# A third Strassen tile pair in the gate projections of a float32 decoder layer, and an earlier start for the first

## The chip, the cores and the metric

The kernel runs on one core of a Trainium2 chip. The metric is the device time of one execution in microseconds (us). Of the kernel before there are three timed runs: 1432.1 us in the median, 1432.09 to 1432.28. Its profiled execution took 1433.02 us, of which the span from the first to the last instruction is 1431.2 us.

## The reference, cut to what matters

All of it is float32, with SEQ = 256 tokens and D_MODEL = 2048. The change lies in the joint projection (its last two parts, the gates) and in how the merge uses them:

```
h = rms_norm(x, ln_mix_w[i])
proj = h @ w_in[i]                      # (256, 2048) @ (2048, 9216)
u_pool, q, f_logit, inp, g, gate_a, gate_b = jnp.split(proj, split_idx, axis=-1)
y_a = multiscale_pool(u_pool, ...) @ w_branch_a[i]
y_b = hgrn2(q, f_logit, inp, g, ...) @ w_branch_b[i]
merged = jax.nn.sigmoid(gate_a) * y_a + jax.nn.sigmoid(gate_b) * y_b
x = x + merged @ w_out[i]
```

After it come a convolutional feed-forward block (`w_up`, `w_down`), a gated embedding (`w_ple_gate`, `w_ple`) and a final norm. Factors in `setup_inputs` scale some of the inputs; they change no shape.

## The kernel before, in words

**Units.** The weights stream through a ring of four buffers (`raw`, `w_hi`, `w_lo`, RING = 4). One *unit* is two row tiles of 128 rows by 512 columns, 512 KB. SyncE issues its DMA; ScalarE rounds it into `w_hi` (`split_hi`, L1119); VectorE subtracts, for the remainder `w_lo` (`split_lo`, L1421); TensorE then takes for each row tile and each of the two blocks of 128 tokens three matmuls, hi x hi, hi x lo and lo x hi (`triple`, L717 to L721; `row_tile`, L661 to L663), 12 in all.

**Slots.** ScalarE's and VectorE's programs are written out slot by slot. In slot s they first split unit s + 3, and then do whatever else is due in that slot, in the order in which it stands in `slot`. A split of unit s + 3 waits until TensorE is through with unit s - 1, whose buffer it takes. Nothing is reordered by a scheduler: each engine works its list in order and waits at semaphores.

**The merge stage.** It has four passes n = 0 to 3 over 512 columns each. A pass from n = 1 on has 24 units, which the text counts from 0 within the pass: units 0 to 15 are the gates (row tile pair i = 0 to 7, for each pair unit 2i of gate a and unit 2i + 1 of gate b), 16 to 19 are branch a, 20 to 23 branch b. The gates accumulate in the PSUM tensor `main`, the branches in `aux`.

**Strassen's scheme.** A tile pair with both gates is a 2 x 2 block product: 2 blocks of tokens, 2 row tiles, 2 column groups. Plain, it takes 8 block products. For the pairs in `GATES_AT` the kernel takes 7 (the Winograd form). Three of them come with the units themselves (`gate_seven`, L789), four use sums of weight tiles and come one pair later (`gate_weight_sums`, L803). The first halves of these follow unit 2i + 2, the second halves unit 2i + 3. Of the products, four (`gate_product`) are gathered over the pairs in the four banks of `aux`: the first is written by `gate_seven`, the second and third (`gate_product(1)` and `(3)`) in the bank pair `aux[0]`. Before the first product of a pass TensorE waits for `gated` (L797), because VectorE must have read branch b's result of the pass before out of `aux`, and before the second for `mT_ready` (L810), because `aux[0]` also holds the transposed `m` of the pass before.

**The sums.** In slot 2i - 2 VectorE forms the four sums of weight tiles in three instructions (`weight_diffs`, L1666, L1668, L1670); ScalarE rounds them in two halves (L1274), and VectorE subtracts in two halves (`sums_lo`, L1695) in the slots 2i and 2i + 1. In these slots the unit 2i + 1 has only one row tile to split (L1117, L1418), since the other is used in sums alone. The sums of activation blocks do not depend on n. They are formed once per pair, during pass 0: GpSimd joins hi and lo (`join_parts`, L2001), VectorE adds four times (`act_sums`), ScalarE rounds and VectorE subtracts. They lie in a buffer with two places.

**Between the passes.** In slot 0 of a pass VectorE multiplies branch b's result with the sigmoid (L1818) and adds both branches to `m_tok` (L1823). TensorE transposes `m_tok` into `aux[0]` after unit 2 (`turn_m`, L714, eight small matmuls). In slot 3 ScalarE copies it out as `mT_hi` (L1331), and VectorE subtracts for `mT_lo` (L1826), which raises `mT_ready`.

**The combination.** When the last Strassen pair is through, ScalarE copies the first product out (L1294), and VectorE makes the shared sums in four additions (`combine_gates`, L1703), then adds them to `main` (`sum_gates`, L1726). TensorE waits for the first of the four before branch a (unit 16), and for all of them before branch b (unit 20).

Of the kernel before, what the change touches and what calls it, by code (L numbers as in the profile page):

```python
# [29 lines left out]
ALU = mybir.AluOpType  # L30
ACT = mybir.ActivationFunctionType
AX_X = mybir.AxisListType.X
F32 = mybir.dt.float32
# [3 lines left out]
P = 128  # L37
# [3 lines left out]
KD = D // P  # L41
# [12 lines left out]
NQ = D // NCOL  # L54
# [8 lines left out]
UK = KD // 2  # L63
# [3 lines left out]
MIX = 10 * UK  # L67
WOUT = MIX + NQ * 2 * (UK + UB)
UP = WOUT + NQ * UK
DOWN = UP + NUP * UK  # L70
# [53 lines left out]


SEVEN_AT = ((5, 8, 11, 14, 17), (5, 8, 11, 14, 17))
GATES_AT = (2, 4)
N_GATES = len(GATES_AT) * (NQ - 1)
SEVENS = [gate_unit(n, i) for n in range(1, NQ) for i in GATES_AT] + [down_unit(p, i) for p in range(2) for i in SEVEN_AT[p]]
SEVEN = {u: q for q, u in enumerate(SEVENS)}  # L130
ACT_SUMS = [0, 1] + SEVENS[N_GATES:]
SUMS_AT = {max(u - 4, DOWN + UK) if f > 1 else MIX + 2 * UK - 2 + 3 * f: f for f, u in enumerate(ACT_SUMS)}
N_SEVEN = [N_GATES + len(SEVEN_AT[0]), len(SEVENS)]
COMBINED0 = 4 * (NQ - 1)

# [66 lines left out]
GATES_COMBINE_AT = [gate_unit(n, GATES_AT[-1]) + 5 for n in range(NQ)]  # L202
# [19 lines left out]
def build(nc, x, x_t, p_t, vecs, convs, w_in, pool_mix_w, w_branch_a, w_branch_b, w_out, w_up, w_down,  # L222
          w_ple_gate, w_ple, ln_final_w, ident_c, levels_c, counts_c, out):
    with ExitStack() as ctx:
# [3 lines left out]
        def sb(name, shape, dt=F32, where=ctx):  # L228
# [63 lines left out]
        mT_hi = sb("mT_hi", [P, KD, SEQ], F32R, mg)  # L292
        mT_lo = sb("mT_lo", [P, KD, SEQ], F32R, mg)
# [15 lines left out]
        a_sums = sb("a_sums", [P, 2, SEQ], F32, ffn)  # L309
        a_sums_hi = sb("a_sums_hi", [P, 2, 4, P], F32R, ffn)  # L310
        a_sums_lo = sb("a_sums_lo", [P, 2, 4, P], F32R, ffn)
# [60 lines left out]
        w_diffs, w_summed, w_sums_hi_ready, w_sums_ready, w_sums_done = map(  # L372
            sem, ("w_diffs", "w_summed", "w_sums_hi_ready", "w_sums_ready", "w_sums_done"))
# [40 lines left out]
        def sums_parts(q):  # L414

            if q < N_GATES:
                return gate_sums_hi, gate_sums_lo
            return w_sums_hi, w_sums_lo

        def down_acc(n, tb):  # L420

# [180 lines left out]
        def _(pe):  # L602
# [121 lines left out]
                return aT_hi[:, k, tb * P:(tb + 1) * P], aT_lo[:, k, tb * P:(tb + 1) * P]  # L724

            def act_sum(q, k):
                return a_sums_hi[:, q % 2, k, :], a_sums_lo[:, q % 2, k, :]

            def ring_tile(u, t):
                return w_hi[:, u % RING, t, :], w_lo[:, u % RING, t, :]  # L730
# [15 lines left out]
            def down_seven(u, p, i, a):  # L746

                q = SEVEN[u - a]
                first, end = i == SEVEN_AT[p][0], i == SEVEN_AT[p][-1]
                pe.wait_ge(lo_full, u + 1)  # L750
                if a == 0:
                    if first:
                        if p:
                            pe.wait_ge(xT_ready, 4 * (2 * NQ + 2))
                        else:
                            pe.wait_ge(z_read, NUP + 1)
                    triple(product(p, 0), *act_block(2 * i, 0), *ring_tile(u, 0), start=first, stop=end)
                    mm = triple(down_acc(2 * p, 0), *act_block(2 * i + 1, 0), *ring_tile(u, 1), start=False, stop=False)
                else:
                    pe.wait_ge(a_sums_ready, q + 3 - N_GATES)  # L760
                    mm = triple(down_acc(2 * p + 1, 0), *act_sum(q, 2), *ring_tile(u, 1), start=False, stop=False)
                mm.then_inc(units_done, 1)

# [25 lines left out]
            def gate_seven(u, n, i, a):  # L789

                q = SEVEN[u - a]
                first, end = i == GATES_AT[0], i == GATES_AT[-1]
                pe.wait_ge(lo_full, u + 1)
                if a == 0:
                    if first:
                        pe.wait_ge(gated, 4 * n)
                    triple(gate_product(0), *x_block_t(2 * i, 0), *ring_tile(u, 0), start=first, stop=end)  # L797
                    mm = triple(main[:, 0, 0, :], *x_block_t(2 * i + 1, 0), *ring_tile(u, 1), start=False, stop=False)
                else:
                    pe.wait_ge(a_sums_ready, q % 2 + 1)  # L800
                    mm = triple(main[:, 1, 0, :], *act_sum(q, 2), *ring_tile(u, 1), start=False, stop=False)
                mm.then_inc(units_done, 1)

# [172 lines left out]
            u = 0  # L976
            first_unit()
            u = 1
# [65 lines left out]
            u = DOWN  # L1044
# [62 lines left out]
        def _(ac):  # L1107
# [153 lines left out]
            def sums_hi(q, part):  # L1261

                if part == 0:
                    ac.wait_ge(a_summed, q + 1)
                    if q > 1:
                        ac.wait_ge(w_sums_done, 2 * (q + N_GATES - 3))
                    ac.activation(a_sums_hi[:, q % 2].rearrange("p k t -> p (k t)"), a_sums[:].rearrange("p k t -> p (k t)"),
                                  ACT.Copy).then_inc(a_sums_hi_ready, 1)
                else:
                    half = part - 1  # L1270
                    ac.wait_ge(w_summed if half else w_diffs, 2 * (q + 1) if half else q + 1)
                    if q:
                        ac.wait_ge(w_sums_done, 2 * (q - 1) + half + 1)
                    ac.activation(sums_parts(q)[0][:, 2 * half:2 * half + 2, :], w_sums[:, 2 * half:2 * half + 2, :],  # L1274
                                  ACT.Copy).then_inc(w_sums_hi_ready, 1)
# [134 lines left out]
        def _(dve):  # L1410
# [274 lines left out]
            def sums_lo(q, part):  # L1685

                if part == 0:
                    dve.wait_ge(a_sums_hi_ready, q + 1)
                    dve.tensor_tensor(a_sums_lo[:, q % 2].rearrange("p k t -> p (k t)"), a_sums[:].rearrange("p k t -> p (k t)"),
                                      a_sums_hi[:, q % 2].rearrange("p k t -> p (k t)").bitcast(F32), ALU.subtract).then_inc(a_sums_ready, 1)  # L1690
                else:
                    half = slice(2 * (part - 1), 2 * part)
                    dve.wait_ge(w_sums_hi_ready, 2 * q + part)
                    hi, lo = sums_parts(q)
                    dve.tensor_tensor(lo[:, half, :], w_sums[:, half, :], hi[:, half, :].bitcast(F32),  # L1695
                                      ALU.subtract).then_inc(w_sums_ready, 1)
# [3 lines left out]
            def add_up(out, a, b):  # L1700

                combines[0] += 1
                return dve.tensor_tensor(out, a, b, ALU.add).then_inc(combined, 1)  # L1703

            def combine_gates(n, part):

                p5, p6, p7 = (gate_product(k) for k in range(1, 4))
                t = [w_sums[:, k, :] for k in range(4)]
                if part == 0:
                    dve.wait_ge(copied, n)  # L1710
                    dve.wait_ge(m_ready, n)
                    add_up(sig_b[:, 1, :], p6, t[0])
                    dve.wait_ge(combined, combines[0])
                    add_up(t[1], p5, sig_b[:, 1, :])
                if part == 1:
                    add_up(t[2], p7, sig_b[:, 1, :])
                    dve.wait_ge(combined, combines[0])
                    add_up(t[3], p5, t[2])
# [35 lines left out]
                    add(x_tok[:, 1, c1], x_tok[:, 1, c1], t[3])  # L1754

            def slot(s):
                if s < UK - LEAD:
                    half_lo(s + LEAD)
                    x_lo(s + LEAD)
                else:  # L1760
                    split_lo(s + LEAD)
                if s in SUMS_AT:
                    act_sums(SUMS_AT[s])
# [6 lines left out]
                        sums_lo(SEVEN[s - k], k + 1)  # L1770
                for n in range(1, NQ):
                    if GATES_COMBINE_AT[n] <= s < GATES_COMBINE_AT[n] + 2:
                        combine_gates(n, s - GATES_COMBINE_AT[n])
                    for k in range(2):
                        if s == merge_slot(n, k) + 1:
                            sum_gates(n, k)
# [168 lines left out]
        def _(pool):  # L1945
# [39 lines left out]
                pool.wait_ge(g_ready, 2 * (g + 1))  # L1985
                pool.tensor_tensor(dec[:, 0, :], dec[:, 0, :], g_tok[:].rearrange("p b n -> p (b n)"), ALU.mult).then_inc(o_gated, 1)

            def join_parts(f, u):

                if f < 2:  # L1990
                    k, hi, lo = 2 * GATES_AT[f], xT_hi, xT_lo
                else:
                    k, hi, lo = u - DOWN - 2 * UD * (u >= DOWN + 2 * UD), aT_hi, aT_lo
                if f == 2:
                    pool.wait_ge(aT_ready, NUP)
                if f:
                    pool.wait_ge(a_sums_ready, f)
                else:
                    pool.wait_ge(yaT_ready, 8)
                    pool.wait_ge(obT_ready, 8)  # L2000
                pool.tensor_tensor(a_sums[:], hi[:, k:k + 2, :].bitcast(F32), lo[:, k:k + 2, :].bitcast(F32),  # L2001
                                   ALU.add).then_inc(a_joined, 1)
# [3 lines left out]
                pool.wait_ge(conv2, plus(j + 1, 1, it))  # L2006
                pool.tensor_tensor(act[:, 0:nf, :], cv[:, 0:nf, :], cv[:, nf:2 * nf, :], ALU.mult).then_inc(prod_u, 1)  # L2007

            for f in range(2):
                join_parts(f, 0)  # L2010
            root(1)
            product(0, 1)
            with pool.Fori(0, NUP - 1) as it:
                product(1, 2, it)
            for f, u in enumerate(ACT_SUMS[2:], 2):
                join_parts(f, u)
            root(2)
            for tb in range(TB):
                pool.wait_ge(end_ms, tb + 1)
# [48 lines left out]
```

## Time and profile before

| | |
|---|---|
| median of 3 runs | 1432.1 us |
| profiled execution | 1433.02 us, span 1431.2 us |
| TensorE (PE) busy | 1420.7 us, 99% |
| PE weight loads busy | 1207.4 us, 84% |
| VectorE (DVE) busy | 1033.4 us, 72% |
| ScalarE (ACT) busy | 774.3 us, 54% |
| GpSimd (POOL) busy | 171.5 us, 12% |
| moved by DMA | 273.47 MB, 191 GB/s in the mean |

Matmuls overlap: a row gives one from its start to its end, and the next starts before that. The distance of their starts tells the pace, not the duration. The same holds, to a smaller degree, for two instructions of VectorE or ScalarE in a row of which neither waits. Idle time in brackets is that of the engine ahead of the instruction, with what ended it.

### The profile page before, as it was taken

Reading aid. Unit: us, or ns where it says so; the run is one execution under the profiler, and the core shown is the slowest. Engines: PE = TensorE matmul, PEld = TensorE weight load, DVE = VectorE, ACT = ScalarE, POOL = GpSimd, SP = SyncE. Lnnn points to the kernel's source line nnn. Section 1 sums busy time; section 2 is a strip of 40 time slices with the busy share of each in tenths; the row PEclk is TensorE's granted clock in tenths of the full one; section 3 lists DMA queues with packets and bytes.
Section 4 is the critical chain, followed back from the end, with each engine's and each line's share of the span. In section 5 each row is a group of like instructions: output and inputs, shape, how many; then the busy total and the mean of one; then the engine's idle time right before and its main releaser. Section 6 shows DMA issues by size and latency. Waiting matters only on the chain.

```text
span 1431.2 us, 19783 instructions
## 1 busy us (share of the span) xinstructions
PE 1420.7 (99%) x7094; PEld 1207.4 (84%) x7094; DVE 1033.4 (72%) x1284; ACT 774.3 (54%) x937; POOL 171.5 (12%) x115
## 2 busy tenths in 40 slices
PE   9999999999999999999999999999999999999997
PEld 7888888888888888888888888888888888888886
DVE  7676777867577765566777777777777888887755
ACT  7555655545454544455555555555555555555644
POOL 0044144100000000000111101111011110000000
PEclk9999999999999999999999999999999999999999
DMA  9655555455665665466656566565665555566663
GB/s 323 199 176 162 161 170 169 147 189 193 193 204 177 220 236 189 156 206 185 190 176 205 177 191 194 173 204 181 192 193 180 202 197 194 174 197 215 231 200 121
DMA packets 190876, 273.47 MB, mean 191 GB/s; under 512 B 11744, under 2 KB 103136, under 8 KB 190688
## 3 DMA queue, kind: packets, MB, share of 16 engines
q1 hardware_dynamic: 190384, 272.30, 59.4%
q8 instruction: 38, 0.62, 0.2%
q10 hardware_dynamic: 432, 0.37, 0.1%
q14 instruction: 22, 0.18, 0.0%
HBM read 270.53 MB, written 2.10 MB: 190 GB/s over the span
## 4 chain that ended last, share of the span: by engine, by line
PE 97%; DVE 1%; issue 0%; DMA 0%; ACT 0%; SPq 0%; ACTq 0%; POOLq 0%; POOL 0%; DVEq 0%
PE aux L839 11%; PE main L839 11%; PE main L661 10%; PE main L663 10%; PE main L662 10%; PE aux L848 6%; PE main L848 6%; PE main L719 5%; PE main L720 5%; PE main L721 5%; PE aux L719 3%; PE aux L720 3%; PE aux L721 3%; PE aux L662 2%; PE aux L661 2%; PE aux L663 2%
## 5 line engine op out<-in xcount | busy, mean ns | idle before, releaser
L1421 DVE TENSOR_TENSOR w_lo<-raw,w_hi 128x1024 fp32r<-128x1024 f32 (+1 forms) x484 | 596.8, 1244 | 337.8 <-ACT w_hi L1119 337.4
L1119 ACT ACTIVATE w_hi<-raw 128x1024 fp32r<-128x1024 f32 (+1 forms) x484 | 508.6, 1052 | 517.3 <-PE main L663 158.4
L661 PE MATMUL main<-w_hi,xT 128*128 128x512 f32 x510 | 201.4, 395 | 0.5 <-DVE w_lo L1883 0.3
L662 PE MATMUL main<-w_lo,xT 128*128 128x512 f32 x510 | 198.6, 389 | 0.0
L663 PE MATMUL main<-w_hi,xT 128*128 128x512 f32 x510 | 198.5, 389 | 0.0
L839 PE MATMUL aux<-xT,w_hi 128*128 128x512 f32 x704 | 169.8, 391 | 0.0
L839 PE MATMUL main<-xT,w_hi 128*128 128x512 f32 x672 | 163.0, 391 | 0.0
L839 PEld LDWEIGHTS aux<-xT,w_hi 128*128 128x128 f32 x704 | 129.3, 188 | 25.3 <-issue 0.3
L839 PEld LDWEIGHTS main<-xT,w_hi 128*128 128x128 f32 x672 | 123.2, 188 | 23.6
L2007 POOL TENSOR_TENSOR act<-cv 128x512 f32<-128x512 f32 (+1 forms) x22 | 71.9, 3267 | 418.8 <-DVE cv L1645 418.8
L661 PEld LDWEIGHTS main<-w_hi,xT 128*128 128x128 f32 x510 | 95.8, 188 | 20.3 <-DVE xT L1448 1.3
L663 PEld LDWEIGHTS main<-w_hi,xT 128*128 128x128 f32 x510 | 95.7, 188 | 20.0
L662 PEld LDWEIGHTS main<-w_lo,xT 128*128 128x128 f32 x510 | 95.9, 188 | 18.8
L848 PEld LDWEIGHTS aux<-xT,w_lo 128*128 128x128 f32 x704 | 90.3, 191 | 3.4
L848 PE MATMUL aux<-xT,w_lo 128*128 128x256 f32 x704 | 91.3, 283 | 0.0
L848 PEld LDWEIGHTS main<-xT,w_lo 128*128 128x128 f32 x672 | 86.4, 191 | 3.5
L848 PE MATMUL main<-xT,w_lo 128*128 128x256 f32 x672 | 87.5, 283 | 0.0
L1645 DVE SCALAR_TENSOR_TENSOR cv<-z,convT,cv 128x255 f32<-128x255 f32 (+1 forms) x172 | 71.7, 479 | 3.0
L1948 POOL TENSOR_TENSOR st<-st,minus_half 128x2 f32<-128x2 f32 (+1 forms) x5 | 3.2, 645 | 490.1 <-DVE st L1479 359.1
L719 PE MATMUL main<-w_hi,xT 128*128 128x512 f32 x150 | 58.6, 391 | 0.0
L721 PE MATMUL main<-w_hi,xT 128*128 128x512 f32 x150 | 58.4, 389 | 0.0
L720 PE MATMUL main<-w_lo,xT 128*128 128x512 f32 x150 | 58.4, 389 | 0.0
(305 smaller groups left out, 2115.3 us busy)
## 6 DMA issues: line engine op xcount, KB each, us to landing
raw<-in_w_up SPq DMA_DIRECT2D x336, 256.0 KB
raw<-in_w_in SPq DMA_DIRECT2D x136, 512.0 KB
raw<-in_w_down SPq DMA_DIRECT2D x84, 512.0 KB
raw<-in_w_out SPq DMA_DIRECT2D x32, 512.0 KB
raw<-in_w_ple_gate SPq DMA_DIRECT2D x32, 512.0 KB
raw<-in_w_branch_a SPq DMA_DIRECT2D x16, 512.0 KB
raw<-in_w_branch_b SPq DMA_DIRECT2D x16, 512.0 KB
raw<-in_w_in SPq DMA_DIRECT2D x15, 256.0 KB, 5.9
```

The lines of the kernel that those rows point to most:

```text
L661: pe.matmul(acc, th, wh, start=first, stop=False)
L662: pe.matmul(acc, th, wl, start=False, stop=False)
L663: return pe.matmul(acc, tl, wh, start=False, stop=end)
L719: pe.matmul(acc, th, wh, start=start, stop=False)
L720: pe.matmul(acc, th, wl, start=False, stop=False)
L721: return pe.matmul(acc, tl, wh, start=False, stop=stop)
L839: mm = pe.matmul(up_acc(j, b), w_hi[:, u % RING, a, b * P:(b + 1) * P], xT[:, k, :, :].rearrange("p h t -> p (h t)"), start=(k == 0), stop ...
L848: mm = pe.matmul(up_acc(j, b)[:, 0:SEQ], w_lo[:, u % RING, a, b * P:(b + 1) * P], xT[:, k, 0, :], start=False, stop=False)
L1119: ac.activation(w_hi[:, u % RING, :, 0:w], raw[:, u % RING, :, 0:w], ACT.Copy).then_inc(hi_full, 1)
L1421: dve.tensor_tensor(w_lo[:, u % RING, :, 0:w], raw[:, u % RING, :, 0:w], w_hi[:, u % RING, :, 0:w].bitcast(F32), ALU.subtract).then_inc(lo ...
L1645: last_op = dve.scalar_tensor_tensor(out=cv[:, b, d:SEQ], in0=z[:, b, 0:SEQ - d], scalar=convT[:, tap, f0(f)], in1=cv[:, b, d:SEQ], op0=AL ...
L2007: pool.tensor_tensor(act[:, 0:nf, :], cv[:, 0:nf, :], cv[:, nf:2 * nf, :], ALU.mult).then_inc(prod_u, 1)
```

## The change

`GATES_AT` becomes (1, 3, 5) instead of (2, 4). So each of the passes 1, 2 and 3 takes three tile pairs with seven block products instead of two, and the first of them is one pair earlier. All that is counted from the table moves with it. A third set of activation sums is kept in a part of `mT` that is not yet in use (`form_parts`), and the sums are formed in slots 11, 14 and 17 of pass 0 instead of 14 and 17. The combination of a pass moves from slots 13 and 14 to 15 and 16. Of its four additions, the first is now alone at the head of slot 15, ahead of the split there; the second stands in slot 15 after the split, the third and fourth in slot 16.

```diff
-GATES_AT = (2, 4)
+GATES_AT = (1, 3, 5)
...
+GATE_FORMS = len(GATES_AT)
...
+SUMS_AT = {MIX + 2 * UK - 5 + 3 * f: f for f in range(GATE_FORMS)}
...
+        def form_parts(f):
+
+            if f == 2:
+                return [t[:, KD - 4:KD - 2, :].rearrange("p k (h t) -> p (k h) t", t=P) for t in (mT_hi, mT_lo)]
+            return a_sums_hi[:, f % 2], a_sums_lo[:, f % 2]
...
@@ combine_gates
                     add_up(sig_b[:, 1, :], p6, t[0])
+                if part == 1:
                     dve.wait_ge(combined, combines[0])
                     add_up(t[1], p5, sig_b[:, 1, :])
-                if part == 1:
+                if part == 2:
                     add_up(t[2], p7, sig_b[:, 1, :])
...
@@ slot (VectorE)
+                if s in GATES_COMBINE_AT[1:]:
+                    combine_gates(GATES_COMBINE_AT.index(s), 0)
                 if s < UK - LEAD:
                     half_lo(s + LEAD)
...
-                        combine_gates(n, s - GATES_COMBINE_AT[n])
+                        combine_gates(n, 1 + s - GATES_COMBINE_AT[n])
```

**VectorE at the start of pass 2**, before. `sig_b` is the gating of branch b, `m_tok` the merged columns, `w_lo` a split (128x512: half a unit), `w_sums` the sums of weight tiles, `gate_sums_lo` their remainder.

```order
L1818 TENSOR_TENSOR sig_b<-aux,sig_b 128x512 [waits gates_ready,units_done]
L1818 TENSOR_TENSOR sig_b<-aux,sig_b 128x512
L1823 TENSOR_TENSOR m_tok<-sig_a,sig_b 128x1024 [waits m_turned,gated]
L1421 TENSOR_TENSOR w_lo<-raw,w_hi 128x1024 [waits hi_full]
L1418 TENSOR_TENSOR w_lo<-raw,w_hi 128x512 [waits hi_full]
L1666 TENSOR_TENSOR w_sums<-raw 128x1024 [waits w_sums_ready]
L1668 TENSOR_TENSOR w_sums<-raw,w_sums 128x512 [waits w_diffs]
L1670 TENSOR_TENSOR w_sums<-raw,w_sums 128x512 [waits w_summed]
L1421 TENSOR_TENSOR w_lo<-raw,w_hi 128x1024 [waits hi_full]
L1826 TENSOR_TENSOR mT_lo<-aux,mT_hi 128x1024 [waits mT_hi_ready]
```

The same place of the changed kernel, whose line numbers are 14 to 17 higher:

```order
L1432 TENSOR_TENSOR w_lo<-raw,w_hi 128x512 [waits hi_full]
L1680 TENSOR_TENSOR w_sums<-raw 128x1024 [waits w_sums_ready]
L1682 TENSOR_TENSOR w_sums<-raw,w_sums 128x512 [waits w_diffs]
L1684 TENSOR_TENSOR w_sums<-raw,w_sums 128x512 [waits w_summed]
L1835 TENSOR_TENSOR sig_b<-aux,sig_b 128x512 [waits gates_ready,units_done]
L1835 TENSOR_TENSOR sig_b<-aux,sig_b 128x512
L1840 TENSOR_TENSOR m_tok<-sig_a,sig_b 128x1024 [waits m_turned,gated]
L1435 TENSOR_TENSOR w_lo<-raw,w_hi 128x1024 [waits hi_full] x2
L1709 TENSOR_TENSOR gate_sums_lo<-w_sums,gate_sums_hi 128x1024 [waits w_sums_hi_ready]
```

It goes on there with one more split, the second `gate_sums_lo`, and then `mT_lo`. The sums of weight tiles now stand ahead of the gating, and both `gate_sums_lo` ahead of `mT_lo`.

**TensorE from the transposes on**, pass 1, in the changed kernel (`a_sums` are sums of activation blocks; the 12 matmuls of unit 4 follow behind the rows shown, and then the first product in `aux[0]`).

```order
L732 MATMUL aux<-w_hi,xT 128x512 [waits gated,lo_full]
L733 MATMUL aux<-w_lo,xT 128x512
L734 MATMUL aux<-w_hi,xT 128x512
L732 MATMUL main<-w_hi,xT 128x512
L733 MATMUL main<-w_lo,xT 128x512
L734 MATMUL main<-w_hi,xT 128x512
L727 MATMUL aux<-ident,m_tok 128x128 [waits m_ready]
L727 MATMUL aux<-ident,m_tok 128x128 x7
L732 MATMUL main<-w_hi,a_sums_hi 128x512 [waits a_sums_ready,lo_full]
L733 MATMUL main<-w_lo,a_sums_hi 128x512
L734 MATMUL main<-w_hi,a_sums_lo 128x512
L732 MATMUL main<-w_hi,xT 128x512 [waits lo_full]
```

Before, the transposes were followed by the 12 matmuls of unit 3 and only then by the wait for `gated`; the same rows followed, and the first product in `aux[0]`, with its wait for `mT_ready`, came two units later than now:

```order
L714 MATMUL aux<-ident,m_tok 128x128 [waits m_ready]
L714 MATMUL aux<-ident,m_tok 128x128 x7
L719 MATMUL main<-w_hi,xT 128x512 [waits lo_full]
L720 MATMUL main<-w_lo,xT 128x512
L721 MATMUL main<-w_hi,xT 128x512
```

## Rows read from the trace of the kernel before

**Rows 1.** The page: engines (part 1), chain that ended last (4), one group (5).

```profile
PE 1420.7 (99%) x7094; PEld 1207.4 (84%) x7094; DVE 1033.4 (72%) x1284; ACT 774.3 (54%) x937; POOL 171.5 (12%) x115
...
PE 97%; DVE 1%; issue 0%; DMA 0%; ACT 0%; SPq 0%; ACTq 0%; POOLq 0%; POOL 0%; DVEq 0%
...
L719 PE MATMUL main<-w_hi,xT 128*128 128x512 f32 x150 | 58.6, 391 | 0.0
```

**Rows 2.** Pass 1: stretch, length, busy PE PEld DVE ACT POOL, clock, DMA, GB/s.

```profile
327.50:392.30 64.80, 64.80 (x291) 53.76 (x290) 47.03 (x48) 32.48 (x34) 0.00 (x0) 1.00 0.61 195
```

**Rows 3.** Timeline, TensorE, start of pass 1: start, duration, instruction.

```profile
327.52 0.39 PE L719 MATMUL main<-w_hi,xT 128*128 128x512 f32 x1
...
332.96 0.39 PE L719 MATMUL main<-w_hi,xT 128*128 128x512 f32 x1
...
335.68 1.03 PE L714 MATMUL aux<-ident,m_tok 128*128 128x128 f32 x8
...
336.47 0.48 PE L719 MATMUL main<-w_hi,xT 128*128 128x512 f32 x1
```

**Rows 4.** Timeline, ScalarE, pass 1.

```profile
327.78 1.06 ACT L1119 ACTIVATE w_hi<-raw 128x1024 fp32r<-128x1024 f32 x1 [1.66 <-PE aux L663]
...
333.22 0.63 ACT L1117 ACTIVATE w_hi<-raw 128x512 fp32r<-128x512 f32 x1 [1.66 <-PE main L721]
...
337.86 1.00 ACT L1331 ACTIVATE mT_hi<-aux 128x1024 fp32r<-128x1024 f32 x1
...
352.53 1.06 ACT L1119 ACTIVATE w_hi<-raw 128x1024 fp32r<-128x1024 f32 x1 [1.72 <-DMA raw<-in_w_in]
...
359.89 0.60 ACT L1294 ACTIVATE w_sums<-aux 128x512 f32<-128x512 f32 x1 [0.24 <-PE main L721]
```

**Rows 5.** Timeline, VectorE, pass 1 from the gating on.

```profile
330.01 1.28 DVE L1818 TENSOR_TENSOR sig_b<-aux,sig_b 128x512 f32<-128x512 f32 x2
331.33 1.23 DVE L1823 TENSOR_TENSOR m_tok<-sig_a,sig_b 128x1024 f32<-128x1024 f32 x1
332.47 1.22 DVE L1421 TENSOR_TENSOR w_lo<-raw,w_hi 128x1024 fp32r<-128x1024 f32 x1
333.88 0.69 DVE L1418 TENSOR_TENSOR w_lo<-raw,w_hi 128x512 fp32r<-128x512 f32 x1 [0.20 <-ACT w_hi L1117]
334.49 1.22 DVE L1666 TENSOR_TENSOR w_sums<-raw 128x1024 f32<-128x1024 f32 x1
...
337.08 1.22 DVE L1421 TENSOR_TENSOR w_lo<-raw,w_hi 128x1024 fp32r<-128x1024 f32 x1
338.89 1.23 DVE L1826 TENSOR_TENSOR mT_lo<-aux,mT_hi 128x1024 fp32r<-128x1024 f32 x1 [0.59 <-ACT mT_hi L1331]
...
341.79 1.22 DVE L1695 TENSOR_TENSOR gate_sums_lo<-w_sums,gate_sums_hi 128x1024 fp32r<-128x1024 f32 x1
342.92 1.22 DVE L1421 TENSOR_TENSOR w_lo<-raw,w_hi 128x1024 fp32r<-128x1024 f32 x1
...
347.77 0.69 DVE L1670 TENSOR_TENSOR w_sums<-raw,w_sums 128x512 f32<-128x512 f32 x1
...
363.76 1.23 DVE L1421 TENSOR_TENSOR w_lo<-raw,w_hi 128x1024 fp32r<-128x1024 f32 x1 [2.85 <-ACT w_hi L1119]
364.90 0.68 DVE L1703 TENSOR_TENSOR sig_b<-aux,w_sums 128x512 f32<-128x512 f32 x1
```

**Rows 6.** Timeline, TensorE restarting behind a wait, early in the program.

```profile
9.26 0.50 PE L661 MATMUL main<-w_hi,xT 128*128 128x512 f32 x1 [0.17 <-DVE xT L1448]
...
9.60 0.40 PE L662 MATMUL main<-w_lo,xT 128*128 128x512 f32 x1
```

**Rows 7.** Timeline, GpSimd, pass 0: the first join of activation blocks.

```profile
289.52 1.30 POOL L2001 TENSOR_TENSOR a_sums<-xT 128x512 f32<-128x512 f32 x1 [18.64 <-DVE yaT_lo L1457]
```

**Rows 8.** Timeline, VectorE, pass 0: the first addition of activation blocks, in slot 14.

```profile
302.81 0.28 DVE L1677 TENSOR_TENSOR a_sums<-a_sums 128x128 f32<-128x128 f32 x1
```

More of the change, by code:

```diff
@@ L130 @@
 SEVEN = {u: q for q, u in enumerate(SEVENS)}
-ACT_SUMS = [0, 1] + SEVENS[N_GATES:]
-SUMS_AT = {max(u - 4, DOWN + UK) if f > 1 else MIX + 2 * UK - 2 + 3 * f: f for f, u in enumerate(ACT_SUMS)}
+GATE_FORMS = len(GATES_AT)
+FORM = [f for n in range(1, NQ) for f in range(GATE_FORMS)] + [GATE_FORMS + q for q in range(len(SEVENS) - N_GATES)]
+N_FORMS = FORM[-1] + 1
+SUMS_AT = {MIX + 2 * UK - 5 + 3 * f: f for f in range(GATE_FORMS)}
+SUMS_AT.update((max(u - 4, DOWN + UK), FORM[q]) for u, q in SEVEN.items() if u >= DOWN)
 N_SEVEN = [N_GATES + len(SEVEN_AT[0]), len(SEVENS)]
@@ L418, in sums_parts, with form_before @@
             return w_sums_hi, w_sums_lo
+        def form_parts(f):
+            if f == 2:
+                return [t[:, KD - 4:KD - 2, :].rearrange("p k (h t) -> p (k h) t", t=P) for t in (mT_hi, mT_lo)]
+            return a_sums_hi[:, f % 2], a_sums_lo[:, f % 2]
+        def form_before(f):
+            return f - 2 if f != GATE_FORMS + 1 else 0
         def down_acc(n, tb):
@@ L726, in act_sum @@
             def act_sum(q, k):
-                return a_sums_hi[:, q % 2, k, :], a_sums_lo[:, q % 2, k, :]
+                hi, lo = form_parts(FORM[q])
+                return hi[:, k, :], lo[:, k, :]
             def ring_tile(u, t):
@@ L759, in down_seven @@
                 else:
-                    pe.wait_ge(a_sums_ready, q + 3 - N_GATES)
+                    pe.wait_ge(a_sums_ready, FORM[q] + 1)
                     mm = triple(down_acc(2 * p + 1, 0), *act_sum(q, 2), *ring_tile(u, 1), start=False, stop=False)
@@ L799, in gate_seven @@
                 else:
-                    pe.wait_ge(a_sums_ready, q % 2 + 1)
+                    pe.wait_ge(a_sums_ready, FORM[q] + 1)
                     mm = triple(main[:, 1, 0, :], *act_sum(q, 2), *ring_tile(u, 1), start=False, stop=False)
@@ L1264, in sums_hi @@
                     ac.wait_ge(a_summed, q + 1)
-                    if q > 1:
-                        ac.wait_ge(w_sums_done, 2 * (q + N_GATES - 3))
-                    ac.activation(a_sums_hi[:, q % 2].rearrange("p k t -> p (k t)"), a_sums[:].rearrange("p k t -> p (k t)"),
+                    if q >= GATE_FORMS:
+                        ac.wait_ge(w_sums_done, 2 * max(r + 1 for r in range(len(SEVENS)) if FORM[r] == form_before(q)))
+                    ac.activation(form_parts(q)[0].rearrange("p k t -> p (k t)"), a_sums[:].rearrange("p k t -> p (k t)"),
                                   ACT.Copy).then_inc(a_sums_hi_ready, 1)
@@ L1688, in sums_lo @@
                     dve.wait_ge(a_sums_hi_ready, q + 1)
-                    dve.tensor_tensor(a_sums_lo[:, q % 2].rearrange("p k t -> p (k t)"), a_sums[:].rearrange("p k t -> p (k t)"),
-                                      a_sums_hi[:, q % 2].rearrange("p k t -> p (k t)").bitcast(F32), ALU.subtract).then_inc(a_sums_ready, 1)
+                    hi, lo = (t.rearrange("p k t -> p (k t)") for t in form_parts(q))
+                    dve.tensor_tensor(lo, a_sums[:].rearrange("p k t -> p (k t)"), hi.bitcast(F32), ALU.subtract).then_inc(a_sums_ready, 1)
                 else:
@@ L1986, in _, with join_parts @@
                 pool.tensor_tensor(dec[:, 0, :], dec[:, 0, :], g_tok[:].rearrange("p b n -> p (b n)"), ALU.mult).then_inc(o_gated, 1)
-            def join_parts(f, u):
-                if f < 2:
+            def join_parts(f):
+                if f < GATE_FORMS:
                     k, hi, lo = 2 * GATES_AT[f], xT_hi, xT_lo
                 else:
+                    u = SEVENS[FORM.index(f)]
                     k, hi, lo = u - DOWN - 2 * UD * (u >= DOWN + 2 * UD), aT_hi, aT_lo
-                if f == 2:
+                if f == GATE_FORMS:
                     pool.wait_ge(aT_ready, NUP)
@@ L2007, in product @@
                 pool.tensor_tensor(act[:, 0:nf, :], cv[:, 0:nf, :], cv[:, nf:2 * nf, :], ALU.mult).then_inc(prod_u, 1)
-            for f in range(2):
-                join_parts(f, 0)
+            for f in range(GATE_FORMS):
+                join_parts(f)
             root(1)
@@ L2014, in _ @@
                 product(1, 2, it)
-            for f, u in enumerate(ACT_SUMS[2:], 2):
-                join_parts(f, u)
+            for f in range(GATE_FORMS, N_FORMS):
+                join_parts(f)
             root(2)
```

## The prediction

> **What bounds the kernel now.** I read the page's engine line and the chain that ended last first [rows 1]: TensorE is busy 99% and carries 97% of the chain, so whatever takes a matmul away, or makes TensorE stand, moves the end by just that much. Then the busy times of one pass of the merge stage [rows 2]: TensorE has no gap there (64.80 of 64.80 us) and runs at a granted clock of 1.00, that is 2.4 GHz; VectorE is busy 47.03 us of it. In the mean it has room, but the mean hides where its work stands. So I went to the timeline of the first units of a pass on each engine [rows 3 to 5]. The reader is to see there how far ahead of TensorE the instruction for `mT_lo` ends.
>
> **The matmuls that go.** Each further Strassen pair saves one block product of eight, three matmuls. Three passes have one pair more: 9 matmuls. Their price is the distance of starts: units 0 and 1 of pass 1 are 24 matmuls and take 332.96 - 327.52 = 5.44 us [rows 3], 0.2267 us each. 9 x 0.2267 = 2.04 us saved.
>
> The group of such matmuls gives 391 ns as the mean of one [rows 1]; nine at that price would be 3.5 us. The Trainium skill, "Perfetto Trace Analysis", in its opening note, calls matmul busy time a bad metric "because matmuls are pipelined"; by that rule the pitch is the price and the 391 ns are not. The trace agrees: 24 in 5.44 us.
>
> **The start of a pass, replayed.** Here the change moves most. I take pass 1 with the times of before; up to 327.52 nothing differs.
>
> TensorE: units 0 and 1 end at 332.96. Unit 2 is now a Strassen unit, 6 matmuls, 1.36 us, then the eight transposes (336.47 - 335.68 = 0.79 us [rows 3]), unit 3 with 3 matmuls (0.68) and unit 4, plain, with 12 (2.72). Then comes the first product in `aux[0]`, behind `mT_ready`. Without a wait it would be reached at 332.96 + 1.36 + 0.79 + 0.68 + 2.72 = 338.51.
>
> VectorE: in slot 0 it splits unit 3, now half a unit. ScalarE starts it at 327.78, as before; half a unit takes it 0.63, and VectorE follows 0.03 later (333.22 + 0.63 against 333.88) [rows 4, 5]. So VectorE starts at 328.44. From there all pitches are read from its own rows [rows 5]: half split 0.61 (333.88 to 334.49), the three sums of weights 2.59 (334.49 to 337.08), gating to `m_tok` 1.32 (330.01 to 331.33), `m_tok`, a split or `gate_sums_lo` 1.14 each (331.33 to 332.47; 341.79 to 342.92). Thus:
> - sums of weights from 329.05, gating from 331.64 to 332.92 (its length 1.28);
> - `m_tok` from 332.96 to 334.19;
> - two splits, `gate_sums_lo`, a split, `gate_sums_lo`: five times 1.14 after 334.10, so `mT_lo` starts at 339.80 and ends 1.23 later, at 341.03.
>
> **Two waits appear.** (1) `gated`: TensorE wants unit 2 at 332.96 and gets the word at 332.92. A restart costs something: the second matmul after a wait starts 0.34 after the first [rows 6], 0.11 more than the pitch, and I add 0.06 from the end of the releasing instruction to the start, so about 0.17 in all (bounds: 0 and the whole 0.34). TensorE is held until 333.09, 0.13 us. (2) `mT_ready`: TensorE arrives at 338.51 + 0.13 = 338.64, and goes on at 341.03 + 0.17 = 341.20. That is 2.56 us of standing. Before, `mT_lo` ended at 338.89 + 1.23 = 340.12, while TensorE, behind the transposes, still had units 3 to 6 to do, 336.47 + 2.72 + 1.36 + 0.68 + 2.72 = 343.95: nobody waited. The transposes do not wait: `m_tok` is ready at 334.19, TensorE reaches them at 333.09 + 1.36 = 334.45. Behind the waiting product stand all later units; ScalarE and VectorE meanwhile catch up, and the time is lost for good.
>
> ScalarE is not later than VectorE here: `mT_hi` takes 1.00 [rows 4] and comes after the transposes (335.24) and behind two roundings of sums and the splits of units 5 and 6. The last of these needs its raw data. A buffer's reload takes from the end of the sums (347.77 + 0.69) to the split (352.53) 4.07 us [rows 4, 5]; here 331.64 + 4.07 = 335.7. So the split of unit 6 is done at 336.8 and `mT_hi` at about 337.7, 2.1 us before VectorE comes to `mT_lo`.
>
> Each of the three passes starts alike (pass 1 gets `m` of pass 0), so the waits cost 3 x (0.13 + 2.56) = 8.07 us. Bounds of the second: `mT_lo` could start no earlier than the seven instructions before it allow, and if all of the restart were free it is 2.39; if the reload were a microsecond later than in rows 4, ScalarE would still be in time. I keep 2.2 to 3.0 for it, and 0 to 0.3 for the first.
>
> **The rest of a pass.** After the wait the pairs 3 and 5 follow at the distance that the pairs 2 and 4 have now. Two pairs take 45 matmuls, 10.2 us; VectorE's work in them is three splits and a half (4.0), sums (2.6) and their remainders (2.3), 8.9 us. It holds the pace, so I cost the third pair at nothing beyond its matmuls. With it VectorE has 4.3 us more per pass, 51.4 of some 67.
>
> **The combination** comes when unit 13 and its second half of sums are done; call this time E. ScalarE's copy ends at about E + 0.7 (its length 0.60 [rows 4]), the first addition (0.68) at E + 1.4, and TensorE wants it for branch a after units 14 and 15, at E + 5.44: 4 us of cover. If it stood behind the split of slot 15 as it does now (363.76, then 364.90 [rows 5]), it would wait for unit 14, ScalarE (1.06) and the split (1.14) and end near E + 5.7, some 0.5 us late per pass with the restart: that is what its new place avoids. The wait for the copy holds the split of unit 18 behind it, which is not wanted before E + 10.9. Cost 0.
>
> **The activation sums** begin in slot 11 of pass 0. GpSimd joins the blocks from 289.52 for 1.30 us [rows 7]; slot 14 has its first addition at 302.81 [rows 8], and three units of 2.72 earlier slot 11 has it at 294.6, so nobody waits. The additions (VectorE, some 2 us a set) fall into slots in which it has only a split of 1.14 in each 2.72. Cost 0. SyncE's wait ahead of the `x` loads in pass 3 is now for unit 13's sums instead of unit 11's, and behind it queue the loads of later units; the next load would in any case wait for a split that needs unit 13. Cost 0.
>
> **Sum.** -2.04 + 8.07 = +6.0 us: 1433.02 becomes 1439.0 for a profiled execution. That one stands 0.9 above the median, which I take as the cost of profiling and leave out: 1432.1 + 6.0 = **1438.1 us**, 0.4% slower. With the bounds: 3 x 2.2 - 2.04 = +4.6 and 3 x 3.3 - 2.04 = +7.9, so 1436.7 to 1440.0.
>
> **Rivals.**
> - *Not slower: `mT_lo` comes in time.* Only the matmuls count: 1432.1 - 2.0 = 1430.1, which is within 0.2% of before. It decides at 338.5: `mT_lo` would have to end 2.5 us earlier than replayed. For it speaks VectorE's idle share in a pass, 17.8 us of 64.8 [rows 2], and that the replay is built on a few pitches. Against it: the chain from 328.44 to 341.03 has no idle time in it that could shrink, and its start hangs on a ScalarE split that TensorE releases. Half of it would leave 1434. Chance 0.08.
> - *The ring runs dry as well.* Each Strassen pair holds two buffers until the sums are formed; before, ScalarE stood 1.72 us for raw data after such a pair [rows 4]. If that wait, or VectorE's longer list, reached TensorE once per pass, it adds 3 x 1.7 = 5.2: 1443.3. Against it: TensorE did not feel it before, and the standing at `mT_ready` lets the others catch up. Chance 0.06.
> - *TensorE's clock falls.* Before, the granted clock is 1.00 in the passes with no gap on TensorE [rows 2]. If after 2.6 us of standing one unit ran at 1.2 GHz, its 12 matmuls would take twice 2.72: three times 2.7 is 8.2 more, 1446.3. How many matmuls would be slow no row shows; one unit is a guess of size. The Trainium skill, "TensorE: Matmul & The Clock Gate", section "HAM oscillation", describes kernels whose waits between groups of matmuls throw the array back to the lower clock each time. No run here shows it at gaps of this length. Chance 0.04.
>
> **How the numbers follow.** The forecast has 0.82, the rivals 0.08, 0.06 and 0.04. About 0.2% (2.9 us) is what a measurement of this kernel can tell from no change. The forecast and the last two rivals are slower by more: 0.92. The first rival gives 0.06 for the same and 0.02 for faster. The range of 8 in 10 is the forecast's own with a little beside it, 1435.8 to 1440.6.
>
> **What would show it.** In the changed profile: 9 matmuls fewer; in each of the passes 1 to 3 one gap on TensorE of about 2.6 us before the first product with `gate_sums_hi` in `aux`, put down to VectorE's `mT_lo`, and one of a tenth or two before the first product of the pass; VectorE without idle time from the half split of slot 0 to `mT_lo`; a first product behind `mT_lo`'s end by 0.1 to 0.2; the same pitch of 0.227 and a clock of 1.00. It is wrong if `mT_lo` ends before TensorE is through with unit 4, if the gap has another releaser (`w_sums`, a raw load, `combined`), or if there are waits at units 16 and 20.

## The result and the profile after

The changed kernel takes 1442.25 us in the median of 6 runs (1440.07 to 1443.71), the kernel before 1432.28 in 6 runs beside it (1432.09 to 1432.56). The ratio is 1.0067, 95% interval 1.0057 to 1.0077: 10 us slower, where 6 were forecast. The runs of before lie within half a microsecond, those of the changed kernel within 3.6, and that turns out to be part of the answer. The profiled execution took 1443.11 us, span 1441.3, 10.1 more than before.

The page of the changed kernel, to be read against [rows 1] (engines, then the chain that ended last):

```profile
PE 1424.4 (99%) x7085; PEld 1208.6 (84%) x7085; DVE 1046.8 (73%) x1304; ACT 780.1 (54%) x944; POOL 172.8 (12%) x116
...
PE 95%; DVE 3%; issue 1%; DMA 0%; ACT 0%; ACTq 0%; POOLq 0%; POOL 0%; DVEq 0%
```

TensorE has 9 matmuls fewer, yet 3.7 us *more* of busy time. No wait explains that; only slower matmuls do. And VectorE now has 3% of the chain instead of 1%.

VectorE at the start of pass 1 in the changed kernel's timeline, against [rows 5]:

```profile
328.24 0.69 DVE L1432 TENSOR_TENSOR w_lo<-raw,w_hi 128x512 fp32r<-128x512 f32 x1 [1.07 <-ACT w_hi L1131]
328.85 1.22 DVE L1680 TENSOR_TENSOR w_sums<-raw 128x1024 f32<-128x1024 f32 x1
...
331.44 1.28 DVE L1835 TENSOR_TENSOR sig_b<-aux,sig_b 128x512 f32<-128x512 f32 x2
332.75 1.23 DVE L1840 TENSOR_TENSOR m_tok<-sig_a,sig_b 128x1024 f32<-128x1024 f32 x1
333.90 2.35 DVE L1435 TENSOR_TENSOR w_lo<-raw,w_hi 128x1024 fp32r<-128x1024 f32 x2
336.17 1.22 DVE L1709 TENSOR_TENSOR gate_sums_lo<-w_sums,gate_sums_hi 128x1024 fp32r<-128x1024 f32 x1
337.30 1.22 DVE L1435 TENSOR_TENSOR w_lo<-raw,w_hi 128x1024 fp32r<-128x1024 f32 x1
338.44 1.22 DVE L1709 TENSOR_TENSOR gate_sums_lo<-w_sums,gate_sums_hi 128x1024 fp32r<-128x1024 f32 x1
339.57 1.22 DVE L1843 TENSOR_TENSOR mT_lo<-aux,mT_hi 128x1024 fp32r<-128x1024 f32 x1
```

There is no idle time from the half split to `mT_lo`, which ends at 340.79, 12.55 us after the half split began. The replay had 12.59.

TensorE in the same stretch, against [rows 3]:

```profile
332.53 0.39 PE L734 MATMUL main<-w_hi,xT 128*128 128x512 f32 x1
332.87 0.47 PE L732 MATMUL aux<-w_hi,xT 128*128 128x512 f32 x1
333.17 0.40 PE L733 MATMUL aux<-w_lo,xT 128*128 128x512 f32 x1
...
338.41 0.39 PE L734 MATMUL main<-w_hi,xT 128*128 128x512 f32 x1
340.94 0.47 PE L732 MATMUL aux<-gate_sums_hi,a_sums_hi 128*128 128x512 f32 x1 [2.14 <-DVE mT_lo L1843]
341.25 0.39 PE L733 MATMUL aux<-gate_sums_lo,a_sums_hi 128*128 128x512 f32 x1
...
342.64 0.63 PE L732 MATMUL main<-w_hi,xT 128*128 128x512 f32 x1
343.07 0.63 PE L733 MATMUL main<-w_lo,xT 128*128 128x512 f32 x1
343.49 0.63 PE L734 MATMUL main<-w_hi,xT 128*128 128x512 f32 x1
```

Read the distances of the starts. Around the first product of the pass they are 0.34 and 0.30 instead of 0.227: 0.18 us lost at `gated` (the view names no releaser here; the run with the gating first, below, shows that it is this wait). Before the first product in `aux[0]` the distance is 2.53, after it 0.31: 2.30 + 0.08 = 2.38 us lost, released by `mT_lo`. And then, from 342.2 to 345.2, it is 0.43. That is the lower level of the clock, 1.2 GHz. The stretches of 5 us behind the three waits (stretch, length, busy times, the granted clock, DMA):

```profile
341.00:346.00 5.00, 5.00 (x15) 4.00 (x16) 4.04 (x5) 1.06 (x1) 0.00 (x0) 0.66 0.16 20
409.40:414.40 5.00, 5.00 (x15) 3.95 (x16) 4.04 (x5) 1.06 (x1) 0.00 (x0) 0.66 0.15 19
477.80:482.80 5.00, 5.00 (x15) 3.94 (x16) 4.02 (x5) 1.06 (x1) 0.00 (x0) 0.66 0.16 19
```

A stretch of 5 us holds 22 matmuls at the full clock; here are 15. One drop costs 1.7 us: TensorE's same instruction (the first product of the pass, its second matmul) stands at 333.17 and 401.57, 68.40 apart, where a pass before took 64.82 (336.47 [rows 3] and 401.29, the first matmul behind the transposes of passes 1 and 2). -0.68 for three matmuls, +0.18, +2.38 and a drop make 3.58, so the drop is 1.70. (A *drop* is from here on one fall of the granted clock to the lower level and back, and its cost what the slower matmuls lose by it.)

### The profile page after: what moved, and what is told of

It reads as the page before. It is cut to its first block, busy times and chain, and to the rows that moved or that the text cites. A ratio compares the mean times of both kernels' runs of the same rounds, so it can differ in the third digit from the quotient of the medians.

```text
span 1441.3 us, 19805 instructions
## 1 busy us (share of the span) xinstructions
PE 1424.4 (99%) x7085; PEld 1208.6 (84%) x7085; DVE 1046.8 (73%) x1304; ACT 780.1 (54%) x944; POOL 172.8 (12%) x116
## 4 chain that ended last, share of the span: by engine, by line
PE 95%; DVE 3%; issue 1%; DMA 0%; ACT 0%; ACTq 0%; POOLq 0%; POOL 0%; DVEq 0%
PE aux L853 11%; PE main L853 11%; PE main L674 10%; PE main L675 10%; PE main L676 10%; PE aux L862 6%; PE main L862 6%; PE main L732 4%; PE main L733 4%; PE main L734 4%; PE aux L732 3%; PE aux L734 3%; PE aux L733 3%; PE aux L675 2%; PE aux L676 2%; PE aux L674 2%
## 5 line engine op out<-in xcount | busy, mean ns | idle before, releaser
L674 PE MATMUL main<-w_hi,xT 128*128 128x512 f32 x510 | 201.4, 395 | 0.3 <-DVE w_lo L1900 0.3
L675 PE MATMUL main<-w_lo,xT 128*128 128x512 f32 x510 | 198.6, 389 | 0.0
L676 PE MATMUL main<-w_hi,xT 128*128 128x512 f32 x510 | 198.5, 389 | 0.0
L1264 ACT ACTIVATE cv<-z,convT 128x256 f32<-128x256 f32 x86 | 44.8, 592 | 23.4 <-DVE z L1650 23.4
L732 PE MATMUL aux<-w_hi,aT_hi 128*128 128x512 f32 x142 | 55.4, 390 | 0.0
L732 PE MATMUL main<-w_hi,aT_hi 128*128 128x512 f32 x142 | 55.3, 390 | 0.0
```

What stands on the lines that cost most here:

```text
L674: pe.matmul(acc, th, wh, start=first, stop=False)
L675: pe.matmul(acc, th, wl, start=False, stop=False)
L676: return pe.matmul(acc, tl, wh, start=False, stop=end)
L732: pe.matmul(acc, th, wh, start=start, stop=False)
```

## The experiments

All were timed beside the kernel before on the same chip; its median was 1432.65 us for the first four and 1432.57 for the last four (21 runs each).

### mT_lo early: the wait taken away

```diff
@@ slot (VectorE), slot 2 of passes 1 to 3
+                    sums_lo(SEVEN[s], 1)
+                    m_lo(n)
                     split_lo(s + LEAD)
@@ slot (ScalarE), slot 3
+                    m_hi(n)
                     split_hi(s + LEAD)
```

> The changed kernel, but ScalarE's copy mT_hi stands ahead of the split of unit 6, and VectorE's order in slot 2 is: first remainder of sums, mT_lo, and only then the split of unit 5. Theory (the wait for mT_lo costs 2.3 us per pass, and the lower clock behind it 1.7 us more): mT_lo ends at about 337.6, a microsecond before TensorE wants it, so wait and clock loss both go; what is left is nine matmuls less (-2.04) and the short wait for the gating (3 x 0.13): 1430.6 us, granted clock 1.00. Rival (the denser Strassen pairs themselves load VectorE, the ring or the array's clock too much): the clock falls in spite of it or another wait appears, 1435 us or more.

Measured: 1431.19 us (1430.96 to 1431.65, 11 runs), ratio 0.9991 (0.9982 to 1.0000), 1.5 us less than before, as was expected, and 11 less than the changed kernel. Its VectorE and its TensorE (two views of the same stretch):

```profile
335.06 1.22 DVE L1716 TENSOR_TENSOR gate_sums_lo<-w_sums,gate_sums_hi 128x1024 fp32r<-128x1024 f32 x1
336.49 1.22 DVE L1781 TENSOR_TENSOR mT_lo<-aux,mT_hi 128x1024 fp32r<-128x1024 f32 x1 [0.21 <-ACT mT_hi L1294]
337.64 2.35 DVE L1442 TENSOR_TENSOR w_lo<-raw,w_hi 128x1024 fp32r<-128x1024 f32 x2
```

```profile
338.46 0.39 PE L734 MATMUL main<-w_hi,xT 128*128 128x512 f32 x1
338.69 0.39 PE L732 MATMUL aux<-gate_sums_hi,a_sums_hi 128*128 128x512 f32 x1
338.91 0.39 PE L733 MATMUL aux<-gate_sums_lo,a_sums_hi 128*128 128x512 f32 x1
```

`mT_lo` ends at 337.71, TensorE comes at 338.69, and the pitch is unbroken. Three Strassen pairs a pass are no load that anything else objects to. The rival falls.

### One instruction later: half of the wait

```diff
@@ slot (VectorE), slot 3 of passes 1 to 3
-                    sums_lo(SEVEN[s - 1], 2)
                     m_lo(n)
+                    sums_lo(SEVEN[s - 1], 2)
```

> The changed kernel, but the second remainder of sums stands behind mT_lo instead of ahead of it, nothing else. mT_lo ends 1.14 us earlier, so TensorE stands 1.2 instead of 2.3 us per pass. If the clock falls only behind the longer standing, all three drops go: 1442.25 - 3.4 - 5.1 = about 1433.7, clock 1.00. If it falls behind any gap: 1438.8, clock 0.996.

Measured: 1434.56 us (1434.33 to 1436.12, 11 runs), ratio 1.0016 (1.0007 to 1.0025), 1.9 us over before. The profiled run has a clock of 0.999 and TensorE's timeline shows

```profile
338.29 0.39 PE L734 MATMUL main<-w_hi,xT 128*128 128x512 f32 x1
339.69 0.47 PE L732 MATMUL aux<-gate_sums_hi,a_sums_hi 128*128 128x512 f32 x1 [1.01 <-DVE mT_lo L1843]
```

The distance is 1.40: 1.17 us lost here and 0.08 at the next. -2.04 + 3 x (0.18 + 1.25) = +2.25 is what the gaps make without drops, and 1.9 was measured. The other ten runs have mean clocks of 0.998 and 0.999, as the kernel before has, so they show no sign of a drop either (one takes 0.001 off); that the eleven still differ by 1.8 us has another cause, which no run looked for. Moving one instruction of 1.14 us saves 7.7 us of the changed kernel's time. Waits alone could give back 3.4, and the rest goes with the clock, whose mean was 0.995 to 0.998 in the changed kernel.

### Pairs 1 and 3: the place without the third pair

```diff
-GATES_AT = (2, 4)
+GATES_AT = (1, 3)
```

> The kernel before with GATES_AT = (1, 3): still two Strassen pairs per pass, but the first at pair 1. Theory (the place of the first pair makes the loss): no matmul is saved, both waits appear as in the changed kernel, 3 x 2.4 = 7.2 us and up to three drops of the clock, 5.1: 1439.5 to 1444.6. Rival (the third pair makes the loss, by VectorE's load): 1432.3, no wait.

Measured: 1442.09 us (1441.55 to 1444.21, 5 runs), ratio 1.0071 (1.0057 to 1.0085). A loss as large as the changed kernel's comes with no third pair and no new combination. That the two are so near is in part chance: here no matmul is saved (2.04 us more), and there was one drop in the profiled execution instead of three. The stretches behind its three waits, each of which cost TensorE 2.3 us at `mT_lo`:

```profile
341.00:346.00 5.00, 4.90 (x22) 4.10 (x23) 4.21 (x5) 1.53 (x2) 0.00 (x0) 1.00 0.14 18
408.50:413.50 5.00, 4.97 (x15) 3.96 (x16) 4.14 (x5) 1.06 (x1) 0.00 (x0) 0.66 0.12 16
477.60:482.60 5.00, 5.00 (x22) 4.14 (x23) 4.10 (x5) 1.60 (x2) 0.00 (x0) 1.00 0.18 20
```

In this profiled execution the clock fell behind one of the three. The same wait at the same place can have a drop behind it or not.

### Written-in gaps of several lengths

```diff
@@ TensorE, behind every eighth unit from unit 7 of pass 1 to the end of the output stage
+                pe.wait_ge(pause, sum(lengths[:pauses.index(u) + 1]))
@@ GpSimd
+            for u in pauses:
+                pool.wait_ge(units_done, u)
+                for r in range(lengths[pauses.index(u)]):
+                    ...
+                    pool.memset(fill[:, 0:312], 0.0).then_inc(pause, 1)
```

> The kernel before, with twelve or more waits of TensorE written in at every eighth unit of the merge and output stages: TensorE waits for GpSimd, which clears a scratch buffer 2, 4 or 6 times in turn after the unit before. Nothing else changes. It measures what standing alone does to the clock. Theory (a gap is enough): behind the longer gaps the granted clock halves for a while and the matmuls' pitch doubles to about 0.43 us for it, some 1.7 us lost for each; behind the shortest it stays. Rival (the drop needs what surrounds it in the changed kernel, so many matmuls on sums or transposes): the clock stays 1.00 throughout, and the loss is the sum of the gaps.

Measured: 1459.29 and 1454.37 us in two runs. By the distances of the starts TensorE lost 2.7 us in each of four gaps, 1.9 in each of four, 1.0 in one; behind the other three of the shortest length no gap is seen, since TensorE had six matmuls on sums left to do between the unit's end and the wait. In the profiled execution, the run of 1459.29 us, the clock fell behind all four long ones and behind none of the others. Two neighbours:

```profile
372.30:377.30 5.00, 5.00 (x22) 4.16 (x23) 2.69 (x4) 1.90 (x3) 0.00 (x0) 1.00 0.47 164
396.90:401.90 5.00, 5.00 (x15) 3.95 (x16) 2.27 (x3) 0.30 (x1) 0.00 (x0) 0.66 0.42 125
```

The first stands behind a gap of 1.9 us, the second behind one of 2.7. No Strassen product stands next to either; the matmuls are plain ones. Standing is enough.

It is not enough every time, though. The second run has the same waits and is 4.9 us shorter, with a mean clock of 0.997 instead of 0.993. Three drops fewer would be 5.1 us, so about one of its four long gaps had a drop behind it. This is an estimate from the time and the clock, since that run has no trace.

### Gaps all alike

The same with `lengths` all 5.

> The kernel before with twelve waits written in as before, but all alike with five clearings of the scratch buffer, so TensorE stands some 2.3 us each time, as in the changed kernel. Gaps of 1.9 us were followed by no drop of the clock and gaps of 2.7 by one each. Theory (at this length it depends on the moment): some but not all of the twelve are followed by the lower clock, and the timed runs differ in their mean clock as those of the changed kernel do. Rival (a fixed length decides): all twelve or none, and all runs alike.

Measured: 1465.27 us (1463.92 to 1466.95, 4 runs). Nine gaps cost TensorE 2.29 to 2.30 us each, within a hundredth of the changed kernel's; three, of which six matmuls on sums covered a part, cost 0.94, with no drop behind them. Behind five of the nine the clock fell, behind four it did not. Two pairs of neighbours from the stretches behind them:

```profile
374.00:379.00 5.00, 4.97 (x15) 3.95 (x16) 1.50 (x3) 0.61 (x1) 0.00 (x0) 0.66 0.40 141
399.80:404.80 5.00, 4.98 (x22) 4.14 (x23) 3.50 (x5) 1.06 (x1) 0.00 (x0) 1.00 0.52 158
446.40:451.40 5.00, 5.00 (x15) 4.00 (x16) 1.45 (x3) 0.32 (x1) 0.00 (x0) 0.66 0.40 135
472.10:477.10 5.00, 4.94 (x22) 4.09 (x23) 3.50 (x5) 1.06 (x1) 0.01 (x1) 1.00 0.51 163
```

The first half of the theory holds: at this length some and not all. The other half, that the runs differ in their clock, is not seen: all four have a mean clock of 0.993, though their times differ by 3 us. Whether it was the same five gaps each time is not on record, and neither is what makes the 3 us.

### The wait filled

```diff
@@ gate_weight_sums (TensorE)
                     if first:
+                        for r in range(9):
+                            pe.matmul(gate_product(2), xT_hi[:, 0, 0:P], obT_hi[:, 0:2, :].rearrange("p k t -> p (k t)"),
+                                      start=True, stop=True)
                         pe.wait_ge(mT_ready, n)
```

> The changed kernel, with nine matmuls of 512 columns on tiles that lie ready written into the place where TensorE waits for mT_lo (their product is overwritten before it is read). They take 9 x 0.227 = 2.04 of the 2.3 us that it stood, so the end of the wait stays where it was, and only the standing goes. Theory (the standing makes the clock fall): clock 1.00, and the time is that of the changed kernel less its drops: about 1438. Rival (the load makes it fall, or the low clock costs nothing): the clock falls as before, 1442.

Measured: 1438.20 us (1437.75 to 1438.68, 5 runs), ratio 1.0041 (1.0027 to 1.0055), clock 0.999. TensorE's timeline:

```profile
338.51 0.39 PE L734 MATMUL main<-w_hi,xT 128*128 128x512 f32 x1
338.74 2.20 PE L826 MATMUL aux<-obT_hi,xT 128*128 128x512 f32 x9
340.97 0.50 PE L732 MATMUL aux<-gate_sums_hi,a_sums_hi 128*128 128x512 f32 x1
```

The product behind `mT_lo` starts 2.46 us after the last useful matmul, as late as in the changed kernel (2.53); only the standing is gone. Nine useless matmuls per pass make the kernel 4 us faster. A pass takes 66.74 us (332.99 to 399.73, first matmul of the first product) instead of 68.40 (332.87 to 401.27), once more 1.7 for one drop. This is the run that separates the two terms: 1438.2 is waits and matmuls, what lies above it is clock. The six runs of the changed kernel fit steps of 1.7 above it: 1440.07 (one drop, 1439.9), 1441.37 and 1441.40 (two, 1441.6), 1443.10, 1443.11 and 1443.71 (three, 1443.3). Their mean clocks go the same way: 0.998, 0.996 twice, 0.995 three times. Only the run of 1443.11 has a trace, which shows its three drops; for the other five the numbers of drops are read from time and clock.

### The gating first

The kernel with `mT_lo` early, and besides:

```diff
@@ slot (VectorE), slot 0 of passes 1 to 3
+                    gate_branch(n, 3)
                 if s + 2 in SEVEN:
                     weight_diffs(s + 2)
```

> The kernel with m early, and besides the two gating instructions of branch b stand ahead of the sums of weight tiles in slot 0 (m_tok stays behind them). Theory: the short wait before the first product of a pass goes (0.11 + 0.07 us each), 3 x 0.18 = 0.5 us less than with m early alone: 1.5 + 0.5 = 2.0 us faster than before, all of the nine matmuls. Rival: the sums come 1.2 us later, so the ring's reload and the splits of units 6 and 7 come later, and what is won is lost again there: no faster than m early alone, or slower.

Measured: 1430.83 us (1430.05 to 1431.58, 11 runs), ratio 0.9988 (0.9979 to 0.9997): 1.7 us faster than before, the best of all. The wait for `gated` is gone from TensorE's timeline:

```profile
332.69 0.39 PE L734 MATMUL main<-w_hi,xT 128*128 128x512 f32 x1
332.92 0.39 PE L732 MATMUL aux<-w_hi,xT 128*128 128x512 f32 x1
333.14 0.39 PE L733 MATMUL aux<-w_lo,xT 128*128 128x512 f32 x1
```

Against `mT_lo` early alone (1.5 faster than before) the further gain of 0.3 us, where 0.5 was expected, is no larger than the medians' own scatter; in the traces a pass takes 64.18 instead of 64.40 us, which is the 0.18 and a little.

### The combination behind the split

The kernel with the gating first, and besides:

```diff
@@ slot (VectorE), slot 15
-                if s in GATES_COMBINE_AT[1:]:
-                    combine_gates(GATES_COMBINE_AT.index(s), 0)
                 ...
                     split_lo(s + LEAD)
...
+                        if s == GATES_COMBINE_AT[n]:
+                            combine_gates(n, 0)
```

> The same as the kernel with the gating first, but the first addition of shared products stands behind the split of slot 15 again, with the second. Theory (as the prediction had it): TensorE then waits some 0.5 us per pass before branch a, so 1.5 us more than with the gating first. Rival: the split is done early enough and its place does not matter, 0.

Measured: 1433.06 us (1432.20 to 1433.25, 11 runs), 2.2 us more than with the gating first (1.5 were expected). VectorE and TensorE in its timeline:

```profile
368.48 1.23 DVE L1442 TENSOR_TENSOR w_lo<-raw,w_hi 128x1024 fp32r<-128x1024 f32 x1 [2.78 <-ACT w_hi L1133]
...
369.62 0.68 DVE L1724 TENSOR_TENSOR sig_b<-aux,w_sums 128x512 f32<-128x512 f32 x1
...
370.36 0.50 PE L674 MATMUL aux<-w_hi,yaT_hi 128*128 128x512 f32 x1 [0.35 <-DVE sig_b L1724]
370.70 0.39 PE L675 MATMUL aux<-w_lo,yaT_hi 128*128 128x512 f32 x1
```

0.51 + 0.11 us are lost before branch a, 1.9 in three passes. So this part of the change does its work.

## Why the prediction was wrong

- **The matmuls that go: right.** 9 fewer, at a pitch of 0.227. The kernel with the gating first is 1.7 us faster than before, against 2.04; in its trace a pass is 0.64 us shorter (64.18 against 64.82), against 0.68.
- **The replay: right.** VectorE's chain took 12.55 us (12.59), and the waits came where they were put, the long one with the releaser that was named. `gated` cost 0.18 (0.13) and `mT_lo` 2.38 (2.56). Together 3 x 2.56 = 7.7 us instead of 8.07. Two small terms were off and hardly show in the sum. The replay let the pass begin as before, at 327.52, and it began 0.20 earlier in this execution, so `mT_lo` ended 0.24 earlier; TensorE was no earlier at the wait, since `gated` cost 0.05 more and the replay left out that the first matmul behind the transposes has 0.09 more than the pitch to the next (0.31, in the trace of before too). And a restart took 0.15 + 0.08 us, not 0.06 + 0.11. The kernel with its wait filled, which has all of this and full clock, is 5.6 us over before, which is -2.04 + 7.7; the forecast was +6.0.
- **The rest of a pass, activation sums, SyncE: right** as a whole, since the kernel with the gating first has them all and shows no further wait, and neither does the changed kernel's own trace. The combination has its cover where it is and would cost 0.6 a pass elsewhere (0.5).
- **The step that failed is the rival "TensorE's clock falls"**, which had a chance of 0.04, and the sum, in which the clock had no term. It fell behind the wait in all three passes of the profiled run, and the six times fit one to three drops per run, 1.7 us each (priced in the rival at 2.7, by a guess of one unit). Together these are 14 drops in 6 runs: 1438.2 + 1.7 x 2.33 = 1442.2; the mean of the six times is 1442.1.

The argument against that rival was that the clock of before is 1.00 in passes with no gap on TensorE. That is no evidence: a kernel in which TensorE never stands can't show what standing does. The Trainium skill, "TensorE: Matmul & The Clock Gate", section "HAM oscillation", which the prediction cited, has the mechanism: waits between groups of matmuls send the array back to the lower clock. In that the traces agree: all 13 drops in the middle of the program in the four traces that have any lie behind a wait, and the same kernel with its wait filled has none. How long TensorE may stand these runs tell for this case alone. Counted in one profiled execution of a kernel each, by what a gap cost TensorE: 0.9 to 1.9 us had no drop behind them (0 of 11), 2.3 us had one in 9 of 15 (3 of 3 in the changed kernel, 1 of 3 with pairs 1 and 3, 5 of 9 written in), 2.7 us in 4 of 4. The last is not a rule: in the other run of that kernel it was about 1 of 4. What decides between a drop and none behind the same gap stays open, since no run here varied it. With these counts a forecast would give each pass a drop at about even odds or better, and its range would reach at least 1443.3, three drops over 1438.2.

## What to carry to other kernels

When a change puts a new wait of two microseconds or more on a TensorE that never waited before, price the wait and the slow matmuls behind it separately, and let the range hold both. (Gaps between 1.9 and 2.3 us were not tried here.) If the wait can't be moved, useless matmuls in its place may pay: here they gave 4 us of 10. When a table entry moves work forward in a hand-ordered program, replay each in-order engine from its last forced start to what the bound engine wants first; the pitches of a timeline gave it here to 0.05 us in 12. The loss lay in what stood ahead of `mT_lo` in VectorE's list, and moving `mT_hi`, `mT_lo` and the gating ahead of what was not yet wanted turned 10 us lost into 1.7 us won.

## What the runs showed of the hardware that was not expected

- A gap of 2.3 us was followed by the lower clock or not, with the same instructions on both sides; the runs of such a kernel spread over 3.6 us, those of kernels without a drop over 0.5 to 1.8. A wide spread of times with hardly changing waits is a reason to look at the clock, but no proof: the four runs with gaps all alike spread over 3.0 us with the same mean clock, and those with half of the wait over 1.8.
- In all 13 drops the lower clock began only after TensorE had gone on, 0.1 to 1.5 us behind the restart: in the changed kernel five matmuls started at about the full pitch from 340.94 on, and the slow ones came from 342.2 on. So the busy time of TensorE rises with a loss that a wait began.
